# Dividing 46 TensorE products of a two-layer block, and moving one operand by 64 bytes

## The reference, cut to what matters

```python
def peer_ffn(h, w_q, sub_k1, sub_k2, expert_u, expert_v):
    ht = h.reshape(T, Dm)
    q = (ht @ w_q).reshape(T, PEER_HEADS, PEER_QDIM)      # 1024 -> 2048: the choice's queries
    s1 = jnp.einsum('thd,nd->thn', q[..., :PEER_HALF], sub_k1)
    ...

def conv_gated_ffn(h, w_up, conv_w, conv_b, w_down):      # called twice, D_FF = 2816
    u = h @ w_up                                          # 1024 -> 5632
    up = jnp.pad(u, ((0, 0), (1, 1), (0, 0)))
    u = up[:, :-2] * conv_w[0] + up[:, 1:-1] * conv_w[1] + up[:, 2:] * conv_w[2] + conv_b
    gate, val = u[..., :D_FF], u[..., D_FF:]
    return (jax.nn.silu(gate) * val) @ w_down             # 2816 -> 1024
```

## Time and profile before

| | us |
|---|---|
| median of 3 runs | 1746.11 (1745.91 to 1750.68) |
| the profiled execution | 1750.57 |
| its span, first to last instruction | 1748.7 |
| TensorE (PE) busy with matmuls | 1737.8 |
| TensorE's weight loads (PEld) | 1533.9 |
| VectorE (DVE) / ScalarE (ACT) / GpSimd (POOL) | 1198.1 / 996.5 / 470.1 |

### The profile page before, as it was taken

How to read it: one execution, slowest core, us unless ns; L and a number is a source line. 1 busy time by engine, 2 the same in 40 slices (tenths; PEclk the granted TensorE clock), 3 DMA queues, 4 the chain that set the end, 5 groups by cost and what they waited for, 6 DMA issues and landing times.

```text
span 1748.7 us, 30169 instructions
## 1 busy us (share of the span) xinstructions
PE 1737.8 (99%) x10556; PEld 1533.9 (88%) x10556; DVE 1198.1 (69%) x2467; ACT 996.5 (57%) x1680; POOL 470.1 (27%) x233
## 2 busy tenths in 40 slices
PE   9999999999999999999999999999999999999998
PEld 8997999899788888888888888877899988889997
DVE  6658859899755555555555555876779965769974
ACT  6578664388455555555555555676466545555554
POOL 1220177198044444444444444000000000000000
PEclk9999999999999999999999999999999999999999
DMA  8561555412655555555556665644555564445562
GB/s 308 201 231 44 190 182 192 146 37 72 200 198 191 190 187 190 190 192 191 189 189 237 238 215 188 239 145 157 196 172 192 184 201 146 170 145 182 182 202 73
DMA packets 84717, 313.67 MB, mean 179 GB/s; under 512 B 9360, under 2 KB 9488, under 8 KB 83216
## 3 DMA queue, kind: packets, MB, share of 16 engines
q1 hardware_dynamic: 82768, 304.18, 51.8%
q10 hardware_dynamic: 1856, 8.23, 1.3%
HBM read 304.78 MB, written 7.60 MB: 179 GB/s over the span
## 4 chain that ended last, share of the span: by engine, by line
PE 95%; ACT 2%; DVE 1%; issue 1%; DMA 0%; POOL 0%; ACTq 0%; DVEq 0%; POOLq 0%
PE bank L861 90%; PE bank L1473 3%; PE bank L1253 1%; DVE wsplit L2185 0%; ACT probs L1851 0%; DMA X<-x 0%; ACT wsplit L1699 0%; PE bank L908 0%; PE bank L1115 0%; PE bank L920 0%; DMA raw<-expert_u 0%; PE bank L1066 0%; POOL wsplit L1668 0%; ACT H L1733 0%; ACT HT L1757 0%
## 5 line engine op out<-in xcount | busy, mean ns | idle before, releaser
L861 PE MATMUL bank<-HT,wsplit 128*128 128x256 f32 (+1 forms) x4928 | 721.5, 304 | 1.1 <-DVE wsplit L2185 0.4
L861 PEld LDWEIGHTS bank<-HT,wsplit 128*128 128x128 f32 x4928 | 672.8, 189 | 54.0 <-issue 4.5
L1668 POOL TENSOR_TENSOR wsplit<-raw,wsplit 128x1024 fp32r<-128x1024 f32 x111 | 277.5, 2500 | 381.3 <-ACT wsplit L2048 381.3
L861 PE MATMUL bank<-wsplit,wexp 128*128 128x512 f32 x1536 | 371.1, 392 | 0.2 <-DVE wexp L2782 0.2
L2048 ACT ACTIVATE wsplit<-raw 128x1024 fp32r<-128x1024 f32 x238 | 240.2, 1053 | 181.8 <-PE bank L861 176.6
L861 PEld LDWEIGHTS bank<-wsplit,wexp 128*128 128x128 f32 x1536 | 280.3, 188 | 56.4 <-DVE wsplit L2757 1.9
L2757 DVE TENSOR_TENSOR wsplit<-raw,wsplit 128x1024 fp32r<-128x1024 f32 x127 | 156.5, 1232 | 108.3 <-ACT wsplit L2048 107.6
L1699 ACT ACTIVATE wsplit<-raw 128x1024 fp32r<-128x1024 f32 x146 | 154.3, 1059 | 99.7 <-PE bank L861 98.6
L2185 DVE TENSOR_TENSOR wsplit<-raw,wsplit 128x1024 fp32r<-128x1024 f32 x124 | 151.6, 1235 | 68.7 <-ACT wsplit L1699 67.4
L2185 DVE TENSOR_TENSOR wsplit<-raw1b,wsplit 128x1024 fp32r<-128x1024 f32 x101 | 121.5, 1221 | 39.8 <-ACT wsplit L1699 39.3
L1699 ACT ACTIVATE wsplit<-raw1b 128x1024 fp32r<-128x1024 f32 x102 | 107.4, 1058 | 69.5 <-PE bank L861 65.2
(11 more groups left out here) (324 smaller groups left out, 2051.6 us busy)
## 6 DMA issues: line engine op xcount, KB each, us to landing
raw<-weights SPq DMA_DIRECT2D x148, 512.0 KB, 4.2
raw<-expert_v SPq DMA_DIRECT2D x127, 512.0 KB, 3.4
raw<-expert_u SPq DMA_DIRECT2D x119, 512.0 KB, 3.7
raw1b<-weights SPq DMA_DIRECT2D x102, 512.0 KB, 4.2
raw1a<-weights SPq DMA_DIRECT2D x48, 512.0 KB, 4.3
early_u<-expert_u SPq DMA_DIRECT2D x5, 512.0 KB, 3.5
raw1a<-expert_u SPq DMA_DIRECT2D x4, 512.0 KB, 4.3
parked<-memT SPq DMA_DIRECT2D x1, 2048.0 KB, 7.3
```

What stands on the lines that cost most here:

```text
L861: ins = pe.matmul(out, lhsT, rhs, start=start, stop=stop, **kw)
L1668: pool.tensor_tensor(wsplit[:, s, 1, :], raw0[:, s, :], f32(wsplit[:, s, 0, :]), ALU.subtract).then_inc(u_lo, 1)
```

## The change

Every `mm3` has three products. At 46 places the change makes four of them. The first one, high by high, is cut in two by columns: one matmul for the first n columns, one for the rest, with the same stationary operand. The other two products stay whole.

- Down stages: in rows k = 1 to 17 of each, at t = h = 0 only, with n from the table `PIECES`: 34 places of 512 columns.
- Up stages: the second tile (n = 24) and the third (n = 32) of each, at k = 1: 4 places of 256 columns.
- The choice's queries: the first tile of each of the 8 groups at k = 1, with n = 24, 32, 40, 48, 16, 56, 64 and 8: 8 places of 256 columns.

Beside that, `ff` becomes two views of one tensor that is 16 floats longer. The first down stage's input begins where it did, and the last one's begins 64 bytes further in. An unused tensor of 16 floats moves `memk_lo` by 64 bytes too.

```diff
+PIECES = (32, 24, 40, 16, 48, 56, 64, 8, 80, 96, 128, 160, 192, 224, 256, 320, 384)
+DIVIDED = {"ffu": {(0, 1): 24, (1, 0): 32}, "pq": {(0, 1): 24, (1, 0): 32, (2, 0): 40, (3, 0): 48, (4, 0): 16, (5, 0): 56, (6, 0): 64, (7, 0): 8}}
...
         late = ExitStack()
+        tensor(late, "room_for_ff", 16)
         memk_lo = tensor(late, "memk_lo", KD, S, dt=F32R)
...
-        ff = tensor(inner, "ff", 2, NF, S, dt=F32R)
+        ff_room = tensor(inner, "ff_room", 2 * NF * S + 16, dt=F32R)
+        ff0, ff1 = (ff_room[:, at:at + 2 * NF * S].rearrange("p (b f s) -> p b f s", b=2, f=NF) for at in (0, 16))
...
+            def mm3_divided(out, left, right, n):
+
+                cols = out.shape[-1]
+                for c in (slice(0, n), slice(n, cols)):
+                    mm(out[:, c], left(0), right(0)[:, c], False, False, skip_group_check=True)
+                mm(out, left(0), right(1), False, False, skip_group_check=True)
+                return mm(out, left(1), right(0), False, False, skip_group_check=True)
...
                 for k in range(KD):
                     wait_turned(fresh, k)
+                    if divide and k == 1:
+                        mm3_divided(out, lambda a: w(a)[:, k, :], lambda b: src[:, b, k, :], divide)
+                        continue
...
                         for h in range(2):
+                            if unit[0] == "ffd" and 0 < k <= len(PIECES) and t == h == 0:
+                                mm3_divided(PS[0][:, :], lambda a: src[:, a, k, tok(0)], lambda b: w(b)[:, 0:512], PIECES[k - 1])
+                                continue
                             products(k, w, t, h)
```

More of the change, by code:

```diff
@@ L962, in wait_turned, with feature_tile @@
                     pe.wait_ge(norm_d, KD * TURNS.index(name) + k + 1)
-            def feature_tile(out, unit, src, fresh=None):
+            def feature_tile(out, unit, src, fresh=None, divide=0):
                 w = tiles_of(weights_of(*unit), k=KD)
@@ L976, in feature_groups @@
                     for c in range(2):
-                        ins = feature_tile(b[:, c * S:(c + 1) * S], units + (2 * g + c,), src, fresh if g == c == 0 else None)
+                        ins = feature_tile(b[:, c * S:(c + 1) * S], units + (2 * g + c,), src, fresh if g == c == 0 else None,
+                                           DIVIDED.get(kind[0], {}).get((g, c), 0))
                     ins.then_inc(bank_full, 1)
@@ L1621, in _ @@
                 feature_groups(("ffu", i), ("ffu", i), range(NF), HT_at(f"ffn{i}"), f"ffn{i}")
-                wide(f"ffd{i}", ("ffd", i), ff, NF, lambda k: pe.wait_ge(conv_m, NF * i + k + 1))
+                wide(f"ffd{i}", ("ffd", i), (ff0, ff1)[i], NF, lambda k: pe.wait_ge(conv_m, NF * i + k + 1))
         @block.gpsimd
@@ L2888, in _ @@
                         link(dve.tensor_tensor(cv[:, g, 0, :], cv[:, g, 0, :], cv[:, g, 1, :], ALU.mult))
-                        parts(ff[:, 0, f - 1, :], ff[:, 1, f - 1, :], cv[:, g, 0, :]).then_inc(conv_m, 1)
+                        parts((ff0, ff1)[i][:, 0, f - 1, :], (ff0, ff1)[i][:, 1, f - 1, :], cv[:, g, 0, :]).then_inc(conv_m, 1)
                 wide_read(f"ffd{i}", X2)
```

## The result

| | before | after |
|---|---|---|
| median | 1746.07 us (9 runs, 1745.91 to 1750.68) | 1756.0 us (9 runs, 1751.53 to 1756.35) |
| ratio of the comparison, 95% interval | 1 | 1.0034 [1.0022, 1.0045] |
| the profiled execution and its span | 1750.57 / 1748.7 us | 1756.26 / 1754.5 us |

A forecast was written before the change was run, and what follows sets the result against it. TensorE was taken to bound the kernel; 3.64 us for the divided places less 0.13 for `memk_lo` gave 3.5 us, on the median of 1746.11 a forecast of 1749.6 us, range 1745.7 to 1755.3.

The forecast's parts named there:

- What bounds the kernel, and that nothing hides the addition: Whole kernel: TensorE busy 1737.8 of 1748.7 us, so every nanosecond added to it is on the path.
- Cost of the pairs: All 46 divided places: two down stages 2.38 us, choice's queries 0.84, up stages 0.42, together 3.64 us.
- the forecast's line: Step of a product of x columns: 120.5 + 0.416 (x - 256) ns, never under 112.
- Where the floor is seen: Down stages: a narrow piece is followed after 107 to 118 ns whatever its width up to about 230.
- rival 2: All 46 places: narrow pieces are cheap, 14 ns each, 0.6 us, 1746.7; sign: 30 ns step behind 24 columns; chance 0.10.
- The down stages' 1.19 us each: The 17 divided places of each down stage add 1.19 us, both stages 2.38 us.
- my second sign of being wrong: The forecast is wrong if whole products change their step beside a divided one.
- The move, taken as 0 with 0.7 us on either side: Last down stage: moving its input 64 bytes costs 0, give or take 0.7 us on 264 products.
- rival 3: Last down stage: the move shifts up to 10.6 ns a product, 2.8 us; 1746.8 or 1752.4; chance 0.10 either way.
- The part for `memk_lo`: Streamed operand `memk_lo` moved 64 bytes: 48 x 2.7 ns, 0.13 us less.
- the likeliest case: Whole run: floor at the weight load, move under 0.7 us; 1749.6 us, own range 1748.5 to 1750.5, chance 0.70.
- The rate of plain float32: Narrow float32r products run at 1.69 ns a column; queries 2.9 us, all 9.1 us, 1755.1; chance 0.10.

The follow-up runs named there:

- e10_half_load: Kernel before with only the down stages' 17 rows each cut at 24 columns, the rest with 64 stationary columns instead of 128; each down stage 0.99 us longer.
- e2_move: Kernel before with only the last down stage's input and `memk_lo` 64 bytes further in, no product divided; 1752.09 us, ratio 1.0011.
- e11_one_80: Kernel before with one divided tile per up stage, the second, cut at 80 columns, nothing moved; 1741.77 us, ratio 0.9960.
- e12_one_80_moved: Kernel before with one tile per up stage cut at 80 columns, plus the 64-byte move of the last down stage's input and `memk_lo`; 1752.27 us, ratio 1.0010.
- e7_up_twelve: Kernel before with twelve divided tiles, pieces of 8 to 128 columns, at the start of each up stage, nothing else; 1745.33 us, ratio 0.9972.
- e9_80_96: Kernel before with two divided tiles per up stage, cut at 80 and 96 columns, nothing moved; 1746.47 us, ratio 0.9981.

## Why the prediction was right, and where it was wrong

- *What bounds the kernel, and that nothing hides the addition.* Right. Every stage grew on TensorE, and no wait came in the stages of the change.
- *Cost of the pairs.* Right in the sum: 0.81 us in the queries against 0.84, 0.20 in an up stage against 0.21. From the starts of the records in the first down stage, the two pieces take more than one whole product by 103 ns at n = 24, 59 at 128 and 5 at 256 (102, 59 and 14 by the forecast's line). Over all 17 places, with what the load behind the narrow second pieces of 192 and 128 columns adds to the whole product there, that is 1.20 us, against 1.19. `e10_half_load` shows its reason, the open weight load.
- *Where the floor is seen.* Wrong. No narrow piece is followed after 107 to 118 ns whatever its width: the next product starts after 27 or 28 ns behind 8 to 64 columns, 58 behind 128, 100 behind 224. The load is waited for inside that next product (its record takes 464 ns behind 24 columns, and the one after it starts 303 ns later). By the signs that I had set down, a step of 30 ns behind 24 columns would have meant rival 2, that narrow pieces are cheap. The sign came, and rival 2 is still out, since the cost lies one product further on. The sign was badly chosen.
- *The down stages' 1.19 us each.* Too small. Without the move each grew by 1.54 us. The whole products behind a divided place were given no cost: they keep steps of 224 to 241 instead of 227 ns, mostly above it, for up to nine products, together 1.54 - 1.20 = 0.34 us a stage. Whole products that change their step beside a divided one were my second sign of being wrong, and it came true, here and in the up stages.
- *The move, taken as 0 with 0.7 us on either side.* This step failed, and by its size: the stationary operand's 64 bytes cost 6.5 ns a product, 1.6 to 1.7 us alone and 1.3 beside the divided products (2.81 - 1.54). I had its bound from a streamed operand's 2.7 ns, and the wider bound stood in rival 3, whose slower side (1752.4) was nearest to what came. Its chance was too low. The part for `memk_lo` was sound: the 144 products of its six tiles took 0.15 to 0.19 us less with the move (the change, `e2_move`) than before, where 0.13 were forecast.
- *Sum.* 3.5 forecast, 5.6 measured level against level: 0.7 from the two down stages, 1.3 from the move. That the 1752.0 us lie in the range is owed to its width, which was there for the rivals. By levels the change gives 1746.1 + 5.6 = 1751.7, too, above the 1750.5 at which the likeliest case's own range ends.
- *Rivals.* The rate of plain float32 would have made the queries 2.9 us longer, and they grew by 0.81. Cheap pieces would have made a down stage 0.24 us longer, and without the move it grew by 1.54. The Trainium skill ("TensorE: Matmul & The Clock Gate", Back-to-back issue gap) has about 25 ns from start to start for up to 64 columns. The trace agrees as to the starts, with 27 ns, and yet the cost of the pair is set by the load. The prediction read that figure as speaking against a floor; the section gives it for a matmul by itself, and says that in a stream of loads and matmuls both set the spacing. By `e10_half_load` a load of 64 columns is 53 ns shorter, and the same page's section on LDWEIGHTS, columns over 1.2 GHz, gives an estimate of 53.
- *The runs' spread.* I read 1745.91 to 1750.68 as noise. They are two steps of TensorE in the up stages. The rows to see it were not in one profile, since both stages of it were at 117.8 ns. But three runs, two together and one 4.6 us apart, were a hint, and the profiled one was the odd one. Of the 9.9 us between the medians, 4.3 come from that.
- *Signs and chances.* The ratio of 1.0034 has an interval of 1.0022 to 1.0045. It is clear of no change, but on neither side of the 0.3% that I took as the bound between "the same" (0.76) and "slower" (0.18), so the runs don't decide between the two.

Open: why a stage of products can run at two steps, what a divided product changes in it, and how the move can keep a stage from the short one. The up stages' products read none of the moved tensors (`memk_lo`, `cv` and `ff`). Two paths were not tested apart. The 24 products right ahead of the first up stage stream `memk_lo`, took 2.93 instead of 2.95 us with the move, and the first steps of the stage differ (122, 117, 118 ns in `e11_one_80`, and 118, 117, 116 in `e12_one_80_moved`). And VectorE writes `cv` and `ff` while an up stage runs. That the move does it rests on profiles and counts of runs from several groups, not on a mechanism.

## What to carry to other kernels

A product narrower than its neighbour's weight load costs the load's uncovered part. Cutting 512 columns cost 103 ns at 24, 59 at 128 and 5 at 256, and the products behind added up to some 40 more (25 at 256). So cut near the middle, or where the cut buys something else. Look for that cost in the product behind the narrow one. Move an operand by a few bytes only with a run that shows its step: here the streamed one gained 2.7 ns by 64 bytes and the stationary one lost 6.5. Where runs of a kernel lie on levels, find the stage that makes them before judging an edit, and compare level with level.

## What the runs showed of the hardware that was not expected

- 1056 products of 256 columns with a weight load each run at 113.3 or at 117.8 ns a product, all else alike. Without a divided product behind the first tile they stay so to the stage's end. A divided product can turn the step in both directions (`e7_up_twelve`, 24 and 48 columns), and so can the waits of a first tile (`e11_one_80`, 113 ns behind them, and `e9_80_96`, 118).
- A narrow product doesn't hold back the start of the next one (27 or 28 ns behind 8 to 64 columns); its open weight load is paid inside that next product (464 ns, and 411 with half the load).
- 76 runs of the kernel before in five groups: 58 with no up stage at 113.3 ns, 18 with one, none with both. The share went from 6 of 9 in one group to 0 of 13 in another.
- The step of a 512-column product by the bytes that its stationary operand lies behind a multiple of 512: 0: 226.9, 32: 233.2, 64: 233.4, 128: 232.4, 256: 226.8, 448: 229.0 ns.
